# Half products of the gates in three parts among the sample steps, one group sooner, with the first merge piece in a space of its own

## The reference, cut to what matters

```python
z = x @ w_in        # [q 16x64 | k 4x64 | v 4x64 | u 512 | memory query 4x64 | 3 gates x 1024]
o_a = sliding_window_attention(q, k, v, sinks)     # window 128, 4 blocks of 128, 4 KV heads
o_b = multiscale_pool(u)
o_c = cross_attention(cq, mem_k, mem_v)            # 4 heads x 64, 256 memory tokens
m = sum_i sigmoid(gate_i) * (branch_i @ w_branch_i)
h = LN1(alpha * x + m @ w_out)
out = LN2(alpha * h + HierMoE(h))
```

## Time and profile before

| | |
|---|---|
| median of three runs | 910.31 us (910.13 to 911.23) |
| the profiled execution's own time | 910.77 us |
| span of the profiled execution | 908.6 us |
| mean granted TensorE clock | 0.956 of full speed |
| PE (TensorE matmul) busy | 837.1 us, 92% of the span, 5420 instructions |
| DVE (VectorE) busy | 530.1 us, 58% |
| ACT (ScalarE) busy | 434.5 us, 48% |
| POOL (GpSimd) busy | 170.5 us, 19% |
| HBM | 200 GB/s over the span |

### The profile page before, as it was taken

One profiled execution on the slowest core, in us unless ns is written; L12 is line 12 of the kernel. 1 busy time (PEld: TensorE's weight loads), 2 busy tenths in 40 slices (PEclk: granted clock), 3 DMA queues, 4 the chain that ended last, 5 costly groups with the idle time before them and its releaser, 6 DMA issues.

```text
span 908.6 us, 13893 instructions
## 1 busy us (share of the span) xinstructions
PE 837.1 (92%) x5420; PEld 742.1 (82%) x5420; DVE 530.1 (58%) x710; ACT 434.5 (48%) x575; POOL 170.5 (19%) x147
## 2 busy tenths in 40 slices
PE   4999988898997999999999997599999999999990
PEld 4999977787885989999999776487888888888870
DVE  3122255646346333444443434779999999999976
ACT  4222232556356242233223214267888788788753
POOL 0086013222122100000000055411121112111104
PEclk9999999999899699999999999599999999999995
DMA  7422200831012113222223363899999999999953
GB/s 293 150 93 92 92 24 25 297 144 48 24 48 88 47 42 132 88 87 87 87 87 139 103 206 129 298 413 397 400 402 389 388 401 402 381 396 402 361 142 94
DMA packets 38143, 179.80 MB, mean 198 GB/s; under 512 B 3919, under 2 KB 11759, under 8 KB 23854
## 3 DMA queue, kind: packets, MB, share of 16 engines
q1 hardware_dynamic: 32486, 159.22, 46.0%
q0 software_dynamic: 5600, 19.99, 7.9%
q10 hardware_dynamic: 16, 0.03, 0.0%
HBM read 164.65 MB, written 16.89 MB: 200 GB/s over the span
## 4 chain that ended last, share of the span: by engine, by line
PE 87%; DVE 6%; DMA 3%; ACT 2%; issue 1%; SPq 0%; DVEq 0%; POOL 0%; POOLq 0%; ACTq 0%
PE ps L1164 7%; PE ps L1165 6%; PE ps L1541 6%; PE ps L1166 6%; PE ps L1543 6%; PE ps L1542 6%; PE ps L1041 4%; PE ps L1042 4%; PE ps L1043 4%; PE ps L1568 3%; PE ps L1570 3%; PE ps L1569 3%; PE ps L1180 2%; PE ps L1182 2%; PE ps L1181 2%; PE ps L1529 2%
## 5 line engine op out<-in xcount | busy, mean ns | idle before, releaser
L2030 DVE TENSOR_TENSOR elo<-eraw,ehi 128x2048 fp32r<-128x2048 f32 x96 | 218.0, 2291 | 25.6 <-ACT ehi L880 23.7
L880 ACT ACTIVATE ehi<-eraw 128x2048 fp32r<-128x2048 f32 x96 | 183.0, 1916 | 27.2 <-PE ps L1543 15.9
L1541 PE MATMUL ps<-ehi,xethi 128*128 128x512 f32 x256 | 103.1, 403 | 3.7 <-issue 2.4
L1543 PE MATMUL ps<-elo,xethi 128*128 128x512 f32 x256 | 101.0, 394 | 0.0
L1542 PE MATMUL ps<-ehi,xetlo 128*128 128x512 f32 x256 | 100.9, 394 | 0.0
L1041 PE MATMUL ps<-xhi,whi 128*128 128x260 f32 x256 | 73.2, 286 | 2.4 <-DVE wlo L1669 2.4
L1164 PE MATMUL ps<-xhi,whi 128*128 128x260 f32 x256 | 74.5, 291 | 0.0
L1165 PE MATMUL ps<-xhi,wlo 128*128 128x260 f32 x256 | 74.0, 289 | 0.0
L1166 PE MATMUL ps<-xlo,whi 128*128 128x260 f32 x256 | 73.9, 289 | 0.0
L1042 PE MATMUL ps<-xhi,wlo 128*128 128x260 f32 x256 | 73.0, 285 | 0.0
L1043 PE MATMUL ps<-xlo,whi 128*128 128x260 f32 x256 | 72.7, 284 | 0.0
(11 more groups left out here) (370 smaller groups left out, 2069.1 us busy)
## 6 DMA issues: line engine op xcount, KB each, us to landing
eraw<-w_gate_in SPq DMA_DIRECT2D x32, 1024.0 KB, 20.3
eraw<-w_up_in SPq DMA_DIRECT2D x32, 1024.0 KB, 20.5
eraw<-w_down_in SPq DMA_DIRECT2D x32, 1024.0 KB, 22.2
raw<-wz_in SPq DMA_DIRECT2D x8, 1024.0 KB, 5.2
late<-wm_in SPq DMA_DIRECT2D x8, 896.0 KB, 4.4
late<-wm_in SPq DMA_DIRECT2D x8, 704.0 KB, 4.0
fraw<-wm_in SPq DMA_DIRECT2D x8, 512.0 KB, 3.5
late<-wo_in SPq DMA_DIRECT2D x4, 1024.0 KB, 4.9
```

Source lines behind the costliest of these rows:

```text
L880: ac.activation(ehi[s % 3][:, :], eraw[s][:, :], ACT.Copy).then_inc(ehi_ok, 1)
L1541: pe.matmul(ps[:, bank, :], hi[:, k, :], ehi[s[j]][:, w], start=k == 0, stop=False)
L1543: last = pe.matmul(ps[:, bank, :], hi[:, k, :], elo[s[j]][:, w], start=False, stop=k == KD - 1)
L2030: ve.tensor_tensor(elo[s % 3][:, :], eraw[s][:, :], ehi[s % 3][:, :].bitcast(F32), ALU.subtract)\
```

## The change

Each fill between groups now stands one group sooner: group g has fill(g+2), and groups 18 and 19 have none. It is cut into three parts, of 3, 3 and 2 of its 8 steps over k (9, 9 and 6 matmuls), which `sample(g)` issues: part 0 behind the sample scores, part 1 behind the small transposes and products (in groups 13 and 15 ahead of them, in 16 and 17 in their middle), part 2 behind `sample_keys`. Fill(0) moves to the front of scores(0), fill(1) stands behind scores(1). Only part 0 waits.

On DVE, `gate_split(0)` moves behind the seventh of the rotations (`r == 6`), and the others from odd groups behind `scaled(g+2)` to even groups right behind `inverse(g+1)`. On ACT, `filled(0)` stands in group 0 behind `exps(1)`, each other `filled` in the group after its fill's, and the last one behind group 19 is gone; `first_split(0)` moves from group 15 to group 13 (`SPLIT_A`), and with it DVE's subtract of that piece from group 16 to group 14.

The first merge piece gets a tile of its own, `first`, in the memory of one `wlo` buffer, where half of the cached memory keys lay before. SP issues it once those keys have been transposed (`kt_ps` at 12) and the last gate piece's hi is made, and no longer waits for fill(15) there; the third part of the first pieces still does, and the second pieces do so too.

```diff
--- before.py
+++ after.py
@@ -72,6 +72,7 @@
 
         raw = [at(f"raw{s}", RING + s * SL, [P, MPW]) for s in range(2)]
         late = [at(f"late{s}", RING + 2 * SL - (2 - s) * 8192, [P, PW]) for s in range(2)]
+        first = at("first", RING + 5 * SL, [P, PW])
         fraw = [at("fraw0", RING + SL, [P, D]), at("fraw1", RING, [P, D])]
         fhi = at("fhi", RING + SL + 4096, [P, D], F32R)
         flo = at("flo", RING + 4096, [P, D], F32R)
@@ -321,7 +322,7 @@
         M_T1, M_T2, M_PV = 13, 15, 16
         M_OUT = M_PV + 1
 
-        SPLIT_A = NKT + 3
+        SPLIT_A = NKT + 1
         LAST = M_OUT + 1
 
 
@@ -330,7 +331,7 @@
 
         def fill_after(g):
 
-            return g + 1 if g < EARLY - 1 else g if g >= EARLY else None
+            return g + 2 if g + 2 < FILLS else None
 
         def wm_parts(i):
 
@@ -455,17 +456,24 @@
 
                 one, two, three = wm_parts(i)
                 n = 2 * i + N_G
+                if i == 1:
+                    sp.wait_ge(prod_ps, EARLY)
                 if i:
                     sp.wait_ge(hi_split, n - 1)
                     sp.wait_ge(lo_split, n - 1)
-                sp.dma_start(late[1][:, 0:MPW - D], one).then_inc(raw_in[1], 16)
-                sp.dma_start(late[1][:, MPW - D:2 * D], two).then_inc(raw_in[1], 16)
+                else:
+                    sp.wait_ge(kt_ps, NKT)
+                    sp.wait_ge(hi_split, N_F + KD - 1)
+                dst = late[1] if i else first
+                sp.dma_start(dst[:, 0:MPW - D], one).then_inc(raw_in[1], 16)
+                sp.dma_start(dst[:, MPW - D:2 * D], two).then_inc(raw_in[1], 16)
                 if i:
                     sp.wait_ge(hi_split, n)
                     sp.wait_ge(lo_split, n)
+                else:
+                    sp.wait_ge(prod_ps, EARLY)
                 sp.dma_start(late[0][:, 0:14 * P], three).then_inc(raw_in[0], 16)
 
-            sp.wait_ge(prod_ps, EARLY)
             for i in range(KD):
                 merge_pieces(i)
             for j in range(4):
@@ -745,7 +753,7 @@
                     ac.wait_ge(kt_ps, NKT)
                 else:
                     ac.wait_ge(sm_ps, 3)
-                ac.activation(whi[n % 2][:, 0:w], late[n % 2][:, 0:w], ACT.Copy).then_inc(hi_split, 1)
+                ac.activation(whi[n % 2][:, 0:w], (first, late[0])[j][:, 0:w], ACT.Copy).then_inc(hi_split, 1)
 
             def gate_split(f):
 
@@ -784,7 +792,9 @@
                     ac.wait_ge(pt_ps, g + 1)
                     ac.wait_ge(o_ps, g)
                     ac.activation(pt[:, 0, :], ps[:, 4, :], ACT.Copy).then_inc(pt_act, 1)
-                m = fill_after(g - 1) if g else 0
+                m = fill_after(g - 1)
+                if g == 0:
+                    filled(0)
                 if m is not None:
                     filled(m)
                     if m % 2 and m < EARLY - 1:
@@ -798,7 +808,6 @@
                     first_split(0)
                 if g == LAST:
                     first_split(1)
-            filled(FILLS - 1)
 
 
             def wo_split(j):
@@ -1165,16 +1174,19 @@
                 pe.matmul(out, cols(wlo[s], q), mh, start=False, stop=False)
                 return pe.matmul(out, cols(whi[s], q), ml, start=False, stop=stop)
 
-            def fill(m):
-
+            def fill(m, part=None):
+
+                if m is None:
+                    return
                 half = m % 2
-                if m:
-                    pe.wait_ge(gate_out, m)
-                else:
-                    pe.wait_ge(row_out, 3)
-                pe.wait_ge(lo_split, N_F + m // 2 + 1 if m < EARLY else N_G + 1)
+                if not part:
+                    if m:
+                        pe.wait_ge(gate_out, m)
+                    else:
+                        pe.wait_ge(row_out, 3)
+                    pe.wait_ge(lo_split, N_F + m // 2 + 1 if m < EARLY else N_G + 1)
                 out = ps[:, 6, 0:TH]
-                for k in range(KD):
+                for k in range(KD) if part is None else range((0, 3, 6)[part], (3, 6, 8)[part]):
                     mh, ml = xk(xhi, k)[half], xk(xlo, k)[half]
                     if m < EARLY:
                         pe.matmul(out, cols(fhi, k), mh, start=k == 0, stop=False)
@@ -1182,7 +1194,8 @@
                         last = pe.matmul(out, cols(fhi, k), ml, start=False, stop=k == KD - 1)
                     else:
                         last = triple(out, A, (m - EARLY) // 2 * KD + k, mh, ml, k == 0, k == KD - 1)
-                last.then_inc(prod_ps, 1)
+                if k == KD - 1:
+                    last.then_inc(prod_ps, 1)
 
             def merge_gates(i):
                 pe.wait_ge(lo_split, 2 * i + N_G + 1)
@@ -1286,8 +1299,10 @@
 
             def sample(i):
 
+                m = fill_after(i)
                 if 1 <= i <= NKT:
                     sample_scores(i - 1)
+                fill(m, 0)
                 if i == 1:
                     pe.wait_ge(rot_mul, 10)
                     for t in range(2):
@@ -1324,6 +1339,8 @@
                                              start=False, stop=b == NS - 1, skip_group_check=True)
                     if i == S_OUT:
                         last.then_inc(sw_ps, 1)
+                if not M_PV <= i <= M_OUT:
+                    fill(m, 1)
                 if i == M_T1:
                     pe.wait_ge(sm_act, 1)
                     for k in range(2):
@@ -1340,6 +1357,8 @@
                         pe.wait_ge(sm_act, 3)
                         pe.wait_ge(cmv_in, 64)
                     for b in range(4 * (i - M_PV), 4 * (i - M_PV) + 4):
+                        if b % 4 == 2:
+                            fill(m, 1)
                         for t in range(2):
                             c = 3 * P + 64 + 16 * t
                             for k in range(2):
@@ -1351,14 +1370,16 @@
                         last.then_inc(sm_ps, 1)
                 if i < NKT:
                     sample_keys(i)
-
+                fill(m, 2)
+
+            fill(0)
             pe.wait_ge(rot_mul, 9)
             pe.wait_ge(roped, 6)
             scores(0)
             rotate(9)
             memory(1, 1)
             scores(1)
-            fill(0)
+            fill(1)
             for g, (kind, b, h) in enumerate(groups):
                 nk = 1 if kind == "swa" and b == 0 else 2
                 pe.wait_ge(sc_nrm, g + 1)
@@ -1394,8 +1415,6 @@
                                                  pt[:, k, (2 * s + j) * P:(2 * s + j) * P + P], start=k == 0, stop=k == 1)
                 last.then_inc(o_ps, 1)
                 sample(g)
-                if fill_after(g) is not None:
-                    fill(fill_after(g))
 
             pe.wait_ge(con_in, 96)
             pe.wait_ge(sw_act, 4)
@@ -1695,6 +1714,13 @@
             split(N_M, 1, PW)
 
 
+            def gate_split(f):
+
+                ve.wait_ge(hi_split, N_F + f + 1)
+                if f:
+                    ve.wait_ge(prod_ps, 2 * f)
+                ve.tensor_tensor(flo[:, :], fraw[f % 2][:, :], fhi[:, :].bitcast(F32), ALU.subtract).then_inc(lo_split, 1)
+
             def rotated(r, t):
                 s = r % 2
                 ve.wait_ge(rot_ps, r + 1)
@@ -1712,6 +1738,8 @@
 
             for r in range(9):
                 rotated(r, ROT[r])
+                if r == 6:
+                    gate_split(0)
             ve.wait_ge(prep, 1)
 
 
@@ -1833,15 +1861,9 @@
 
             def merge_split(n, w):
                 ve.wait_ge(hi_split, n + 1)
-                ve.tensor_tensor(wlo[n % 2][:, 0:w], late[n % 2][:, 0:w], whi[n % 2][:, 0:w].bitcast(F32), ALU.subtract)\
+                ve.tensor_tensor(wlo[n % 2][:, 0:w], (first if n == N_G else late[n % 2])[:, 0:w], whi[n % 2][:, 0:w].bitcast(F32), ALU.subtract)\
                   .then_inc(lo_split, 1)
 
-            def gate_split(f):
-
-                ve.wait_ge(hi_split, N_F + f + 1)
-                if f:
-                    ve.wait_ge(prod_ps, 2 * f)
-                ve.tensor_tensor(flo[:, :], fraw[f % 2][:, :], fhi[:, :].bitcast(F32), ALU.subtract).then_inc(lo_split, 1)
 
             scaled(0)
             row_max(0)
@@ -1855,7 +1877,6 @@
             for r in range(2):
                 last = ve.tensor_copy(cqp[64 * r:64 * r + 64, :, r, :], z[64 * r:64 * r + 64, ZC:ZC + 2, SEQ:T])
             last.then_inc(qs_ok, 1)
-            gate_split(0)
             inverse(0)
             scaled(1)
             row_max(1)
@@ -1869,12 +1890,12 @@
                     ve.tensor_copy(pt[:, 1, :], ps[:, 5, :]).then_inc(pt_dve, 1)
                 if g + 1 < NGR:
                     inverse(g + 1)
+                if g % 2 == 0 and g < EARLY - 2:
+                    gate_split(g // 2 + 1)
                 if g:
                     sample(g - 1)
                 if g + 2 < NGR:
                     scaled(g + 2)
-                if g % 2 and g < EARLY - 1:
-                    gate_split(g // 2 + 1)
                 sample_norm(g)
                 if g + 2 < NGR:
```

## The result

The changed kernel took 924.91 us in the median of five runs (913.79 to 926.17) against 910.31 (909.78 to 914.57) for the kernel before: a ratio of 1.0128 [1.0066, 1.0191], slower. (Ratios go by the means of the executions, not by the medians; a bracket is the 95% interval.) The spread is the surprise. In all 25 executions of the changed kernel that were timed in this study, 14 lay between 913.3 and 917.0 us and 11 between 924.5 and 932.4, with nothing between; both kinds came on the same chip. The shares differed from chip to chip (1 of 5, 10 of 12, 2 of 6 and 1 of 2 were of the shorter kind). The comparisons count both kinds. The kernel before has no second kind: nearly all its executions lie between 909 and 916.

The account below looks back on a forecast made before the run. TensorE was taken to bound the kernel, by its waits and slow clock. Waits +4.1 and clock -3.3 gave +0.8 on the profiled 910.77, 911.6; less 0.46 for that execution, 911.1, range 906.0 to 916.5 (8 in 10).

Parts of the forecast that it names:

- Start: Scores(0) to group 0: fill(0) fills a hole, fill(1) waits 4.1 us; together -0.7, plus 1.5 for one clock fall.
- Even groups: Waits for flo, held by POOL: 1.3 us in groups 2, 4, 10, 12 and 1.45 in 6; net +1.5.
- Fill(16): Group 14: TensorE waits 4.8 us for wlo, which DVE makes only behind rest(14).
- Merge: Before merge_branches(0): TensorE waits for wlo of the second merge piece, made behind rest(19); +2.8 us.
- Group 19: Transposes 19 wait for POOL's normalising, no longer hidden by a fill: +1.1 us.
- Rival (b): Even groups: POOL does not hold flo, five waits fall to 0.4 us without clock falls; about 904; chance 0.08.
- How often the even groups fall: Clock in even groups: one third of five groups fall, 1.7 us each; +2.8 (0 to 8.5).
- rival (c): Waits for flo take the clock down in every even group: +6.5 us, 916.8; decides from the third; chance 0.27.
- the end: Groups 18 and 19, without fills: waits +3.9 us; clock down until into merge_branches(0), 1.7 to 6, taken as +3.1.
- the first merge piece: Its earlier split moves fill(16) to group 14: waits net +2.8 us, and a clock fall of 1.7 to 3.4, +2.3.
- Rival (a): The clock holds: only the two longest waits (4.1 and 4.8 us) bring falls; 905.2; chance 0.13.

Follow-up runs that it names:

- run 34: Not a run or kernel: "run" is the verb in "groups 14 to 19 and the first products of the merge run 34 us at 1.2 GHz".
- gate 0 first: Changed kernel with ACT's copy of fill(0) out of bank 6 moved ahead of exps(0): 918.7 us, ratio 1.0087.
- fill(16) later: Changed kernel with fills 16 to 18 one group later (groups 15 to 17) and fill(19) behind the sample step of group 19: 917.8 us, ratio 1.006.
- the three together: Changed kernel with POOL's normalising held until flo is made, filled(0) ahead of exps(0), and fills 16 to 18 one group later: 898.9 us, ratio 0.9853.
- one wait kept busy: Changed kernel with unread matmuls in one wait only: ahead of the merge 925.9 us, ahead of fill(16) 920.0, ahead of fill(1) 922.2.
- the two kernels with the last groups kept busy: Changed kernel with unread matmuls in the waits of groups 18, 19 and the merge: 920.9 us; with 36 ahead of fill(16) too: 916.4.
- the three edits with their last waits filled, the best version: Changed kernel with POOL held for flo, filled(0) before exps(0), fills 16 to 18 later, and unread matmuls in waits of groups 15, 18, 19: 896.1 us.
- The kernel with POOL behind flo: Changed kernel with POOL's normalising of the next group held until DVE has made flo, in groups following a split: 908.8 us, ratio 0.9973.
- the kernel with the end alone kept busy: Changed kernel with 20 unread matmuls ahead of merge_branches(0) only: 925.9 us (917.2 to 930.5).

## Why the prediction was wrong

The forecast was 911.1 (906.0 to 916.5), no change; the median was 924.91. The shorter kind lies in the range, but at 914 it is slower by 0.3 to 0.4%, so that "no change", within 0.2%, is wrong for it too.

**The waits were right.** Start: scores(0) follow fill(0) with 0.18 us of waiting, and fill(1) waits 4.21 (4.1 forecast). It comes at 165.32 instead of 166.5, because that whole profile runs 1.25 earlier from before the groups on: the seventh rotation's first step on DVE stands at 148.31, at 149.56 before, whose profile has a low stretch from 18.8 us that this one has not. Even groups: 1.14 to 1.27 recorded, 1.4 to 1.5 with the 0.25; the forecast was 1.3 to 1.45. Fill(16): 4.67 + 0.25 against 4.8. Merge: 2.70 + 0.25 against 2.8. Group 19: 1.0 against 1.1. In all, the waits from 152 to 335 us add up to 21.6 us, where those before add up to 15.1, and to some 17.4 with the 2.3 that its low clock hid: +4.2, for which the sum had +4.1. Rival (b) is out: POOL holds the subtract, and taking the hold away brought some 5 us, from 914 in the shorter kind to 908.8, in two comparisons on different chips. On this the Trainium skill (GPSIMD Engine Reference, Specifications) agrees with the runs as to contention; that it is a hold of the whole instruction, 0.95 us here, the runs add.

**The clock failed, in three steps of the sum.** The one that failed first is "How often the even groups fall": one third of five groups, +2.8. In the first profile, groups 2, 4, 8, 9 and 10 hold 17 us at 1.2 GHz, a loss of 8.5, which is the far end of that term's own bounds and the price of rival (c), with 2 of its falls in groups 8 and 9, where there is no wait for flo. With 1.7 behind fill(1), 1.7 in group 14 and 1.7 ahead in the merge, 13.6 are lost in place of the 9.7 that the sum had (1.5 + 2.8 + 2.3 + 3.1), and of the 13.0 lost before nothing was won. The three other profiles of the shorter kind lose the same 13.6, with 3.4 of it behind fill(1) and 6.8 in groups 4 to 12. Part of the step was that the sum took off all the falls of the kernel before, those of groups 8 and 9 too, without a reason for these: in three of the four profiles 6.8 us fell there again. From the same instant on (1.25 off) the start of the merge is 3.5 us later, with the stretch behind it 5.2. The profiled time is 3.0 later, for 1.25 of it is that earlier start, and some 0.9 are won behind the merge's start, where no code differs.

The two that failed worst are **the end** ("between 1.7 and 6; +3.1") and, with it, **the first merge piece** ("1.7 to 3.4; +2.3"): in the profile of the longer kind, the one that there is of the changed kernel (11 of the 25 executions were of that kind by their times), groups 14 to 19 and the first products of the merge run 34 us at 1.2 GHz, more than the 20.5 there before. By my estimate that costs some 13 us (9.1 more than in the shorter kind up to the merge, 1.7 that the shorter kind loses there itself, 2.4 in the merge) in place of the 5.4 of the two terms; in the shorter kind it was 3.4. I had taken the stretch from 292 us to be removed with its waits, and priced the new waits one by one, each with the fall behind it. What I missed is that a fall there is not followed by dense work. In seven profiles (the longer kind's, and those with gate 0 first, fill(16) later, the three together, and one wait kept busy) a low stretch begins in group 17, whose sample step has few columns, and lasts 17 to 21 us, through groups 18 and 19, to the start of the merge or into it. In the changed kernel these two groups have no fill any more and 4.5 us of work in 9.9. With their waits filled it lasted 6.8 us, as the two kernels with the last groups kept busy show, and in the profile of the three edits with their last waits filled it was absent. In the shorter kind the fall comes at 335.2, when the dense products have begun, and lasts 3.4. Thus one and the same program is worth 914 or 925.

The rival on the other side, (c), had the right direction and part of the place. The bound from which it should decide, the third such group, was reached (groups 2, 4 and 10); but groups 6 and 12 waited as long, 1.27 and 1.15 us, with no fall behind it, and its 916.8 leaves out the end. Rival (a) is out: the clock fell behind waits of 1.14 us. The Trainium skill (TensorE: Matmul & The Clock Gate, Why this matters for your kernels) names long idle gaps; here a single wait of 1.14 us came ahead of a fall (188.08 and 205.62 in the first profile).

**What stays open.** What decides where a fall begins was not found. The low stretches begin at other instants in each execution (at fill(1): between 164.1 and 166.7 in the five profiles of the changed kernel), and whether the kind that an execution becomes follows from that, the runs don't show. The kernel with POOL behind flo has the last groups of the change unaltered. Ten of those twelve were not long; whether the one of 914.5 us at the lower clock was its longer kind is not known, for no profile of it was taken, and that it is spared for good is not shown. That filling the first wait alone, or that of group 14 alone, made all executions longer than the shorter kind belongs here: their profiles have the stretch of 20.5 us from group 17 on, and why is not shown. Which falls among groups 0 to 13 go with which wait was not tested one by one.

## What to carry to other kernels

When a change trades waits for others of nearly the same sum, price the clock over the whole stretch that follows, not behind each wait: look for places as empty as groups 18 and 19 here (4.5 us of work in 9.9), for in seven profiles a fall that came ahead of them lasted through them. Take several profiles and read the spread of the executions, since one profile may show only the lucky kind; here four of five did. A wait that can't be removed can be filled with matmuls that nobody reads; in this kernel, with the three longest waits filled, none of twelve executions was of the longer kind, and with one of them filled all 17 took more than 917 us.

## What the runs showed of the hardware that was not expected

A subtract of two SBUF tiles on DVE that starts 0.8 us into a POOL tensor operation of 1.89 us is held nearly until that ends: it ends 1.08 behind it, and its record grows from 1.22 to 2.17 us; letting POOL wait for the short DVE operation instead cost TensorE nothing there, as POOL's result was ready at 192.63 and needed at 194.12. The same program runs in two times 11 us apart at equal waits, by the granted clock: 0.959 and 0.943 over the span, with 27.3 and 54.6 us at 1.2 GHz from fill(1) into the merge. And 20 dense matmuls in a row at the end did not raise a clock that was already low: they took 4.51 us in the profile of the kernel with the end alone kept busy, where 20 of them ahead of group 15, at full clock, took 2.65 in the best version.
